# A two-layer encoder trunk in float32 on one core: the opening's transfers, the first norm's spread, the bias table and the warm-up products rearranged

## The reference

```
for i in range(2):
    h = rmsnorm(x, norm_mix_g[i])                       # x * rsqrt(mean(x*x) + 1e-6) * g
    x = x + (even_mixer(h) if i == 0 else diff_attention(h))
    x = x + square(relu(rmsnorm(x, norm_ffn_g[i]) @ w_ff1[i])) @ w_ff2[i]
return rmsnorm(x, norm_final_g)
```

## Time and profile before

| | before |
|---|---|
| median of 3 runs | 2164.21 us (2163.47 to 2164.64) |
| the profiled execution | 2164.72 us, its span 2162.9 us |
| mean granted TensorE clock | 0.999 |
| PE busy | 2153.2 us of 2162.9 |
| DVE, ACT busy | 1389.1 us, 1021.8 us |
| DMA | 408.92 MB, mean 189 GB/s |

### The profile page before, as it was taken

One profiled execution on the slowest core, in us unless ns is written; L12 is line 12 of the kernel. 1 busy time (PEld: TensorE's weight loads), 2 busy tenths in 40 slices (PEclk: granted clock), 3 DMA queues, 4 the chain that ended last, 5 costly groups with the idle time before them and its releaser, 6 DMA issues.

```text
span 2162.9 us, 30895 instructions
## 1 busy us (share of the span) xinstructions
PE 2153.2 (100%) x11160; PEld 1837.7 (85%) x11160; DVE 1389.1 (64%) x1945; ACT 1021.8 (47%) x1442; POOL 15.9 (1%) x31
## 2 busy tenths in 40 slices
PE   9999999999999999999999999999999999999998
PEld 7888888888888888888888888888888888888887
DVE  6777756755764665675577777657646656755754
ACT  6444445544543443454445445454434434444543
POOL 1000000000000000000000000000000000000000
PEclk9999999999999999999999999999999999999999
DMA  9544456555555555555544444545555555555553
GB/s 355 205 164 168 158 184 223 186 195 186 192 194 195 186 188 192 191 194 182 187 176 175 175 159 173 195 175 194 194 193 180 192 195 194 183 195 185 193 194 117
DMA packets 63347, 408.92 MB, mean 189 GB/s; under 512 B 6724, under 2 KB 12356, under 8 KB 15262
## 3 DMA queue, kind: packets, MB, share of 16 engines
q1 hardware_dynamic: 60046, 402.46, 52.1%
q10 hardware_dynamic: 2656, 3.44, 0.5%
q0 software_dynamic: 560, 1.84, 0.2%
HBM read 405.58 MB, written 2.14 MB: 189 GB/s over the span
## 4 chain that ended last, share of the span: by engine, by line
PE 98%; DMA 1%; issue 0%; ACT 0%; SPq 0%; DVE 0%; POOL 0%; POOLq 0%; DVEq 0%; ACTq 0%
PE acc L1073 32%; PE acc L1077 16%; PE ps_scores L1106 7%; PE ps_scores L1107 7%; PE ps_scores L1105 7%; PE ps_v L1105 4%; PE ps_v L1106 4%; PE ps_v L1107 4%; PE acc L1106 2%; PE acc L1107 2%; PE acc L1105 2%; PE ps_aux L1105 2%; PE ps_aux L1106 2%; PE ps_aux L1107 2%; PE ps_o L1164 1%; PE ps_scores L1164 1%
## 5 line engine op out<-in xcount | busy, mean ns | idle before, releaser
L661 DVE TENSOR_TENSOR w_lo<-raw,w_hi 128x1024 fp32r<-128x1024 f32 x744 | 908.4, 1223 | 520.7 <-ACT w_hi L363 518.0
L363 ACT ACTIVATE w_hi<-raw 128x1024 fp32r<-128x1024 f32 x744 | 787.1, 1058 | 633.4 <-PE ps_scores L1107 253.9
L1073 PE MATMUL acc<-gx,w_hi 128*128 128x512 f32 x3008 | 947.0, 396 | 0.0
L1077 PEld LDWEIGHTS acc<-gx,w_lo 128*128 128x128 f32 x3008 | 565.0, 188 | 133.2
L1077 PE MATMUL acc<-gx,w_lo 128*128 128x256 f32 x3008 | 591.3, 278 | 0.0
L1073 PEld LDWEIGHTS acc<-gx,w_hi 128*128 128x128 f32 x3008 | 460.2, 189 | 2.2 <-DVE w_lo L661 0.2
L1105 PE MATMUL ps_scores<-w_hi,mid 128*128 128x512 f32 x640 | 249.5, 390 | 0.0
L1107 PE MATMUL ps_scores<-w_hi,mid 128*128 128x512 f32 x640 | 249.0, 389 | 0.0
L1106 PE MATMUL ps_scores<-w_lo,mid 128*128 128x512 f32 x640 | 249.0, 389 | 0.0
L370 ACT ACTIVATE copied<-acc 128x256 f32<-128x256 f32 x188 | 72.0, 383 | 316.3 <-PE acc L1077 316.3
L694 DVE TENSOR_TENSOR head<-acc,copied 128x256 f32<-128x256 f32 x188 | 79.8, 424 | 176.2 <-ACT copied L370 174.7
(11 more groups left out here) (198 smaller groups left out, 1629.0 us busy)
## 6 DMA issues: line engine op xcount, KB each, us to landing
raw<-weights_dram SPq DMA_DIRECT2D x372, 1024.0 KB, 4.8
raw<-opening_dram SPq DMA_DIRECT2D x6, 512.0 KB, 8.9
x<-x_tok_dram SPq DMA_DIRECT2D x2, 1024.0 KB, 15.1
bias<-bias_line SPq DMA_DIRECT2D x2, 1024.0 KB, 9.6
bias<-bias_line ACTq DMA_DIRECT2D x2, 1024.0 KB, 8.7
bias<-x_fm_dram SPq DMA_DIRECT2D x6, 256.0 KB, 8.9
bias<-bias_line SPq DMA_DIRECT2D x2, 512.0 KB, 5.9
bias<-final_gain_dram POOLq DMA_DIRECT2D x1, 1024.0 KB, 7.0
```

Source lines behind the costliest of these rows:

```text
L363: act.activation(w_hi[:, n % RING, :], raw[:, u % RAW_SLOTS, part * HALF:(part + 1) * HALF], ACT.Copy).then_inc(hi_ready, 1)
L661: dve.tensor_tensor(w_lo[:, n % RING, :], raw[:, u % RAW_SLOTS, part * HALF:(part + 1) * HALF], w_hi[:, n % RING, :].bitcast(F32), ALU.sub ...
L1073: pe.matmul(acc[w % 2][:], w_hi[:, n % RING, j * P:(j + 1) * P], gx[:, kt, :], start=kt == 0, stop=False)
L1077: ins = pe.matmul(acc[w % 2][:, SEQ:], w_lo[:, n % RING, i * P:(i + 1) * P], gx[:, kts[i], 0:SEQ], start=False, stop=kts[i] == KT - 1)
```

## The change

- The pieces in which SP requests the opening: steps 4 and 5 come as two pieces instead of one.
- 10 warm-up products instead of 12.
- The table, its extra row and the one-hot matrix are joined on the host into one array `positions` (33 x 532). ACT's queue fetches it with one DMA, behind the two that stood there; three DMAs on POOL's queue go. `bias_rows` follows kt 1 instead of kt 2, and ACT's copy of its result step 3 instead of 5.
- The identity, the lambdas and `subln` are requested by POOL only once DVE has split 8 of the 16 opening steps.
- SP requests the token rows alternately with the units: unit 4, tokens 0, unit 5, tokens 1, instead of unit 4, unit 5, tokens 0, tokens 1.
- ACT squares the token rows in two operations of 1024 columns for each half instead of four of 512. The two unused partial sums are set to zero. ACT's second pair of squares, and DVE's adding of the parts, come after the split of half 11 instead of before.
- On PE `spread` of the first norm moves from the first half of unit 5 to its second, and `group_maps` from the second to the first. The two-column product for lambda leaves `group_maps` and follows head 0's scores, in the middle of unit 6.

```diff
-CHUNKS = ((0, 1), (1, 2), (2, 3), (3, 4), (4, 6), (6, 8), (8, 10), (10, 12), (12, 14), (14, 16))
+CHUNKS = ((0, 1), (1, 2), (2, 3), (3, 4), (4, 5), (5, 6), (6, 8), (8, 10), (10, 12), (12, 14), (14, 16))
-WARM = 12
+WARM = 10
...
-        one_hot = bias[0:BUCKETS + 1, 1, :, :].rearrange("b t k -> b (t k)")
+        table_rows = bias[0:BUCKETS + 1, 1:3, :, :].rearrange("b h t k -> b (h t k)")
+        one_hot, tab = table_rows[:, 0:LINE], table_rows[:, LINE:LINE + HEADS]
...
+        first_squares_out = mid[:, 0:2, :].rearrange("p k c -> p (k c)")
...
@@ SP
-            load(4)
-            load(5)
             for t in range(QT):
+                load(OPEN + t)
                 sp.dma_start(x[:, t, :], x_tok[:, t, :]).then_inc(tokens_landed[t], 16)
...
@@ POOL
+            pool.memset(token_parts[:, :, 2:COL_GROUPS], 0.0)
...
-            pool.dma_start(tab[0:BUCKETS, :], table).then_inc(tab_landed, 16)
-            pool.dma_start(tab[BUCKETS:BUCKETS + 1, :], a_head_row).then_inc(tab_landed, 16)
-            pool.dma_start(one_hot, onehot).then_inc(tab_landed, 16)
+            pool.wait_ge(open_lo, KT // 2)
             pool.dma_start(ident[:], identity).then_inc(small_landed, 16)
             pool.dma_start(lam_in[:], lambdas).then_inc(small_landed, 16)
             pool.dma_start(sub_gain_in[:], subln).then_inc(small_landed, 16)
...
@@ ACT
             act.dma_start(raw_open[:, 1:2, :], opening[:, 1:2, :]).then_inc(open_landed[1], 16)
+            act.dma_start(table_rows[:, 0:LINE + HEADS], positions).then_inc(tab_landed, 16)
...
-                if k == 5:
+                if k == 3:
                     act.wait_ge(line_ready, 1)
...
                 act.wait_ge(tokens_landed[t], 16)
-                for g in range(COL_GROUPS):
-                    square_tokens(COL_GROUPS * t + g, t, g)
+                for g in range(2):
+                    if t or g:
+                        act.wait_ge(sq_done, COL_GROUPS // 2 * (2 * t + g))
+                    act.activation(first_squares_out, x[:, t, g * D // 2:(g + 1) * D // 2], ACT.Square,
+                                   scale=1.0 / math.sqrt(D), accum_out=token_parts[:, t, g:g + 1]
+                                   ).then_inc(sq_done, COL_GROUPS // 2)
...
             first_squares(0)
             split_hi(10)
+            split_hi(11)
             first_squares(1)
-            split_hi(11)
...
@@ DVE
             split_lo(10)
+            split_lo(11)
             token_stats(N_MIX0)()
-            split_lo(11)
...
@@ PE
-                pe.wait_ge(tab_landed, 16 * 3)
+                pe.wait_ge(tab_landed, 16)
...
                 ins.then_inc(map_ready, 1)
+
+            def lambda_sums():
+
                 pe.wait_ge(lam_steps, 1)
                 pe.wait_ge(rstd_ready, N_MIX0 + 1)
                 pe.matmul(ps_aux[:, 0:2], ones[:], lam_prod[:], start=True, stop=True).then_inc(lam_sum_ready, 1)
...
-                if kt == 2:
+                if kt == 1:
                     bias_rows()
...
-                    narrow(u + 1, w + 1, hooks=({4: [spread(N_MIX0)]}, {4: [group_maps]}))
+                    narrow(u + 1, w + 1, hooks=({4: [group_maps]}, {4: [spread(N_MIX0)]}))
...
-                    values_quarter(0, group, group, u + 2, h % V_HEADS0, middle=[scores(0, 2 * h + 2, h)])
+                    values_quarter(0, group, group, u + 2, h % V_HEADS0,
+                                   middle=[scores(0, 2 * h + 2, h)] + ([lambda_sums] if h == 0 else []))
```

More of the change, by code:

```diff
@@ L109, with trunk @@
 Y_ACT = ((0, 0, D // 2), (1, 0, 6 * P))
-def trunk(nc, first_x, x_fm, x_tok, opening, weights, final_gain, subln, lambdas, table, w_fnet, onehot, a_head_row,
+def trunk(nc, first_x, x_fm, x_tok, opening, weights, final_gain, subln, lambdas, positions, w_fnet,
           channel_dft, position_dft, identity, out):
@@ L151, in trunk @@
         neg_lam = sb("neg_lam", [P, 1])
-        tab = sb("tab", [BUCKETS + 1, HEADS])
         pos_dft = sb("pos_dft", [P, QT, 2, SEQ])
@@ L1239, in bias_rows @@
             def bias_rows():
-                pe.wait_ge(tab_landed, 16 * 3)
-                pe.matmul(scores_flat[0][0:HEADS, :], tab[:], one_hot, start=True, stop=True).then_inc(line_ready, 1)
+                pe.wait_ge(tab_landed, 16)
+                pe.matmul(scores_flat[0][0:HEADS, :], tab, one_hot, start=True, stop=True).then_inc(line_ready, 1)
             def group_maps():
@@ L1570 @@
         "lambdas": np.ascontiguousarray(np.concatenate([lambda_q1, lambda_k1, lambda_q2, lambda_k2]).T),
-        "table": np.ascontiguousarray(rel_bias_table),
+        "positions": np.concatenate([onehot, np.concatenate([np.asarray(rel_bias_table), a_head_row])], axis=1),
         "w_fnet": np.ascontiguousarray(np.asarray(w_fnet)[0]),
-        "onehot": onehot, "a_head_row": a_head_row, "channel_dft": channel, "position_dft": position,
+        "channel_dft": channel, "position_dft": position,
         "identity": identity,
```

## The result

| | before | after |
|---|---|---|
| median | 2164.2 us (16 runs) | 2168.09 us (16 runs, 2166.93 to 2169.72) |
| ratio | | 1.002, 95% interval 1.0013 to 1.0026 |
| the profiled execution, its span | 2164.72, 2162.9 us | 2167.93, 2165.7 us |

A forecast was written before the change was run, and what follows sets the result against it. PE was taken as the bound, with an equally long DVE chain behind the factor's copy. Terms -0.43, -1.23, -0.14, +3.37, +0.2 gave +1.8 on the median 2164.2: 2166.0 us, range 2162.6 to 2167.9.

The forecast's parts named there:

- the part on the rule: PE's pause before unit 6: skill's rule says long gaps lower the clock, rows show none after 1.23 us; sum kept +1.8.
- What bounds the kernel, DVE's chain and the new wait: Before unit 6: DVE's 4.6 us from factor copy to `v_split` outlasts PE's 1.9; PE idles 3.4 us, costing +3.37.
- The wait for the factor goes: Before the spread: PE's wait for POOL's factor, 1.23 us, disappears because the spread starts later, at 40.87.
- The scores meet no second wait, the lambda product follows them: After unit 6's first half: keys at 48.93, scores at 49.19, no wait; lambda product behind them costs 0.2 us.
- The sum without the clock: Whole kernel, with the clock staying at its upper level: +1.8 us, 2166.0 against the median.
- the third rival: Pause before unit 6: clock falls, losing 2.7 us (2168.7), or 2167.5 if back after 3 us; chance 0.12.
- Warm-up, -0.43: Opening: 10 warm-up products instead of 12 win 0.43 us, between 0 and 0.86, if the clock rises when it did.
- the opening's other edits, 0: Opening: smaller pieces, earlier `bias_rows`, table on ACT's queue give 0, between -0.3 and +0.3; POOL's later requests cost 0.
- Token rows and squares, factor ready at 37.3 us: Before the spread: second-half tokens still at 33.81, two squares ready 0.6 us earlier, POOL ends at 37.3 (36.4 to 37.9).

The follow-up runs named there:

- b_spread_only: Kernel before with only the swap of spread and maps and the move of the lambda product; 2168.22 us.
- f3: f1 with head 0's values operations put ahead of later splits on DVE, and ACT in the matching order; 2162.59 us.
- a_fill12: Changed kernel with 12 more 128 x 128 products of ones by ones on PE ahead of unit 6; 2166.55 us.
- b_warm10: Kernel before with 10 warm-up products; 2164.32 us.
- a_warm12: Changed kernel with 12 warm-up products again; 2167.88 us.
- a_spread_back: Changed kernel with the spread back in unit 5's first half and the maps in its second; 2165.26 us.
- f2: Changed kernel with maps and spread both at the first hook of unit 5; 2164.24 us.
- f1: Kernel before with 10 warm-up products, later 1024-column squares, lambda product behind the scores, maps then spread at unit 5's first hook; 2163.62 us.
- a_fill6: Changed kernel with 6 more products of ones by ones on PE ahead of unit 6; 2166.62 us.
- first group: Kernel before, unchanged, in the first of four groups of runs beside the experiments; median span 2162.4 us.
- third group: Kernel before, unchanged, in the third of four groups of runs beside the experiments; median span 2162.6 us.

## Why the prediction was wrong

The step that failed is the choice at the end of the part on the rule: "by the rows it stays at +1.8". The clock fell. Point by point:

- *What bounds the kernel, DVE's chain and the new wait.* Right, in place and size: 3.4 us forecast, 3.38 measured; copy of the factor 41.63 forecast, 40.77 measured. Of that difference 0.41 us is the opening (0.84 won, 0.43 forecast), the rest tenths of a microsecond in each step behind it. b_spread_only and f3 show the chain from both sides.
- *The wait for the factor goes.* Right; the longer one in front of unit 6 stands in its place.
- *The scores meet no second wait, the lambda product follows them.* Right: it costs 0.14 us (50.63 to 50.77), forecast 0.2. In a_fill12, where no low clock hides them, the scores start at 48.40, again without a wait.
- *The sum without the clock.* +1.8 us forecast; a_fill12, which has everything but the fall, has +1.8 in its median span, but only +0.92 at unit 6's second half and +1.2 in the span by the single traces. So the fit is known only to within most of a microsecond, and some of it may be luck.
- *The clock.* This was the third rival, with a chance of 0.12 and a price of 2.7, or 1.5 if the clock came back after 3 us. It came back after 3.4, and a_fill12 prices the fall at 1.54: within 0.1 of the rival's lower price. From the only pause in the trace, 1.23 us without a mark, I reasoned to one three times as long. The trace bore out neither side there, and the rule of the Trainium skill (TensorE: Matmul & The Clock Gate, section "HAM oscillation — how this bites in real kernels"), that a long enough gap between bursts sends the clock back, was the only thing that spoke of such a pause; the traces agree with it (clock 0.50 from 46.0 to 49.4, behind an idle 3.38 us). The price I took from the opening, 5.4 us at half speed, was too high.
- *Warm-up, -0.43, and the opening's other edits, 0.* The total was near, its parts were not. The opening as a whole gives 0.84 us between the two traces and about 0.5 by the means of all. The two products, which were to give all of it, show nothing in the medians of b_warm10 and a_warm12. The term took the clock to rise at the same moment as before; in these traces that moment varies.
- *Token rows and squares, factor ready at 37.3 us.* Wrong, and without effect here. ACT starts on tokens 1 at 34.63 instead of 33.81, and POOL ends at 37.37 + 0.72 = 38.09, still 2 us ahead of the spread. With the spread in its old place it makes PE's wait 2.1 us (a_spread_back). Why they come late stays open; f2's trace has them at 33.86.
- *Missing from the sum:* 0.4 us outside the span. The changed kernel has it in 12 of 16 runs, and every kernel with its opening (the a_ kernels, f2) in some, 2.2 to 2.5 us instead of 1.8 or 1.9. None of the five edits tried alone brings it, but one run of f3 has it too (2.4), which has neither the joined array nor the eleven pieces nor POOL's wait. Its cause stays open. So does 0.2 us that PE of the changed kernel loses between 100 and 300 us.

So of the 3.9 us, about 1.8 are the pause net of what the opening won, 1.6 the clock, and 0.4 to 0.5 lie outside the span.

## What to carry to other kernels

An idle stretch on the bounding engine is the place where a wait shows, not always the one that sets the time: before moving the producer later, follow its consumer to the next point at which the bounding engine needs something, and count the work in between on both engines. Here DVE had 4.6 us of work and PE 1.9. Fill such a wait with work that stands behind it (f1), and shorten the chain by putting first what is wanted first (f3). And count such a pause of PE twice, once for itself and once for the clock: here one of 3.4 us lost the clock in most runs, and by the spans one of about 2 us did in a third of them.

## What was not expected of the hardware

- The clock fell half a microsecond after the pause had ended, not in it (46.0 against 45.51, and between 46.8 and 47.0 against 46.04), and stayed low for 3.4 us in both traces. In a_warm12 it fell 0.2 us after unit 6's start at 45.62, and was low for as long:

```profile
45.63:45.83 0.20, 0.20 (x1) 1.00 0.60 205
45.90:49.20 3.30, 3.30 (x9) 0.50 0.72 298
```

- Whether it falls varies from run to run. By their spans, the pause of 3.4 us made it fall in 15 of the changed kernel's 16 runs (one span, 2164.5, is that of a_fill12) and in 9 of b_spread_only's 11, a pause of about 2 us in 4 of 11 (a_spread_back) and 3 of 11 (a_fill6), and the 1.2 us of the kernel before in none of the 33 runs of the first group, whose spans end at 2163.3 (in the third group one of 2164.1 stands apart). In traces it is seen in three kernels: the changed one, b_spread_only and a_warm12. Five runs of the changed kernel, with spans of 2167.0 to 2167.4, lost another 1.3 us that no trace shows.
- Fewer warm-up products at the lower level of the clock bought nothing that the medians show. In b_warm10's trace the first matmul is 0.6 us earlier and unit 4 0.1 us.
- The moment at which the clock first rises differs from trace to trace of one opening: by the changed kernel's second 512-column matmul, 0.33 us behind the first, and by a_fill6's third, 0.43 behind the second.
